# Forgetting attention of a hybrid decoder step: prompt scores made in two layouts, with a pair's row maxima fetched one pair ahead

## What is computed

```python
s = jnp.einsum('bqhd,bkhd->bhqk', qb, k, preferred_element_type=F32) * scale
s = s + jnp.swapaxes(cqb, 1, 2)[..., :, None] - ckT[:, :, None, :]
s = jnp.where((kpos[None, :] <= qpb[:, None])[None, None], s, -jnp.inf)
p = jax.nn.softmax(s, axis=-1)
return jnp.einsum('bhqk,bkhd->bqhd', p.astype(v.dtype), v)
...
y = (o * jax.nn.silu(z)).astype(h.dtype) @ w_out
```

## Time and profile before

| | us |
|---|---|
| median of three runs (lowest, highest) | 2239.72 (2234.27, 2247.66) |
| profiled execution | 2248.77 |
| its span, first to last instruction | 2247.0 |
| TensorE busy in the span | 1930.5 (86%) |
| VectorE, ScalarE, POOL busy | 1129.9, 563.5, 349.8 |
| mean granted clock of TensorE | 0.907 |

### The profile page before, as it was taken

How to read it: one execution, slowest core, us unless ns; L and a number is a source line. 1 busy time by engine, 2 the same in 40 slices (tenths; PEclk the granted TensorE clock), 3 DMA queues, 4 the chain that set the end, 5 groups by cost and what they waited for, 6 DMA issues and landing times. The chain is left out here.

```text
span 2247.0 us, 39897 instructions
## 1 busy us (share of the span) xinstructions
PE 1930.5 (86%) x15120; PEld 1416.0 (63%) x15120; DVE 1129.9 (50%) x1810; ACT 563.5 (25%) x1253; POOL 349.8 (16%) x401
## 2 busy tenths in 40 slices
PE   4999999999999788999999996877877768768798
PEld 3876877777787566877877774544444434344475
DVE  4444534544563687677677763333334333333423
ACT  4211121121121421111111111333433334233431
POOL 0000000000000034544445442011011010110010
PEclk9999999999999898999999997568889788687899
DMA  4111111111111479999999997247678676685761
GB/s 136 38 44 48 43 40 56 35 49 47 39 49 38 161 232 308 343 312 341 348 325 330 317 323 253 105 154 248 218 212 258 224 233 225 203 257 181 276 243 71
DMA packets 218393, 413.65 MB, mean 184 GB/s; under 512 B 18593, under 2 KB 129858, under 8 KB 218014
## 3 DMA queue, kind: packets, MB, share of 16 engines
q1 hardware_dynamic: 148764, 222.15, 30.6%
q0 software_dynamic: 51648, 180.71, 23.5%
q10 hardware_dynamic: 17874, 9.27, 1.4%
HBM read 370.85 MB, written 41.94 MB: 184 GB/s over the span
## 5 line engine op out<-in xcount | busy, mean ns | idle before, releaser
L1180 DVE STREAM_TRANSPOSE kt<-k_raw 128x1024 f32<-128x1024 f32 x256 | 310.8, 1234 | 145.7 <-DMA k_raw<-in_cache_k_dram,k_idx 120.0
L347 POOL DMA_INDIRECT k_raw<-in_cache_k_dram,k_idx x256 | 259.4, 1013 | 444.4 <-DVE kt L1180 284.6
L765 PE MATMUL ps_a<-h_hi,w_hi 128*128 128x512 f32 x656 | 265.7, 405 | 1.7 <-DVE w_lo L1017 1.7
L766 PE MATMUL ps_a<-h_lo,w_hi 128*128 128x512 f32 x656 | 258.7, 394 | 0.0
L767 PE MATMUL ps_a<-h_hi,w_lo 128*128 128x512 f32 x656 | 258.6, 394 | 0.0
L1693 DVE TENSOR_REDUCE pp_nm<-ps_a 128x1 f32<-128x128 f32 (+3 forms) x64 | 48.5, 758 | 306.4 <-PE ps_a L1421 306.4
L1017 DVE TENSOR_TENSOR w_lo<-w_raw,w_hi 128x1024 fp32r<-128x1024 f32 x97 | 109.1, 1124 | 171.3 <-ACT w_hi L594 169.0
L1443 PE MATMUL b<-con,p_p 128*128 128x128 f32 x432 | 98.4, 347 | 102.7 <-DVE p_p L1701 48.4
L765 PE MATMUL ps_b<-h_hi,w_hi 128*128 128x512 f32 x384 | 157.2, 409 | 0.0
L766 PE MATMUL ps_b<-h_lo,w_hi 128*128 128x512 f32 x384 | 152.1, 396 | 0.0
L767 PE MATMUL ps_b<-h_hi,w_lo 128*128 128x512 f32 x384 | 152.0, 396 | 0.0
(11 more groups left out here) (291 smaller groups left out, 3131.8 us busy)
## 6 DMA issues: line engine op xcount, KB each, us to landing
v_pg<-in_cache_v_dram SPq DMA_DIRECT2D x256, 512.0 KB, 5.1
w_raw<-in_w_in_pool_dram SPq DMA_DIRECT2D x32, 512.0 KB
w_raw<-in_w_in_attn_dram SPq DMA_DIRECT2D x32, 512.0 KB
w_raw<-in_w_out_pool_dram SPq DMA_DIRECT2D x16, 512.0 KB
s_scr<-ss_st ACTq DMA_DIRECT2D x64, 128.0 KB
s_in<-s_scr POOLq DMA_DIRECT2D x16, 512.0 KB, 5.0
d_sb<-decay POOLq DMA_DIRECT2D x32, 256.0 KB, 6.9
z_scr<-x_st SPq DMA_DIRECT2D x8, 528.0 KB, 4.6
```

Of the source, the lines that this page charges most:

```text
L347: pool.indirect_dma_start(k_raw[:, k, :], None, cache_rows, bass.IndirectOffsetOnAxis(ap=k_idx[:, u, k:k + 1], axis=0)).then_inc(k_full[k] ...
L765: nc.tensor.matmul(ps, ah, bh, start=j == 0, stop=False)
L766: nc.tensor.matmul(ps, ah, bl, start=False, stop=False)
L1180: V.transpose(kt[u % 2][:, :, 32 * k:32 * k + 32], k_raw[:, k, :].rearrange("p (i c) -> p i c", c=32)).then_inc(dve_kt, 1)
```

## The change

- The scores of a pair are made twice. `query_rows` makes them as before, queries on partitions, only for the row maxima, and one pair ahead: while pair `b` is worked, the rows of pair `b + 1` are made and reduced (`row_max`, `max_columns`). `keys_turned` makes them with keys on partitions, with a 67th row that adds the negated maximum of each query; ScalarE's `prompt_exp` is then an exponential without bias or sum, and its result `pt_x` is at once the moving operand of `prompt_values`. `QBLOCKS`, `prompt_turn`, `prompt_evac` and `prompt_norm` are gone.
- The steps go over key blocks 0 to 7; step `s` has the queries from 128 s on, in parts of up to 512 columns. Both kinds of scores pass through a ring of four banks. The values' sums stand in `o_ps` (two banks) for the whole pair.
- The maxima get into the query tile by `max_row`: TensorE turns 16 columns of maxima (`max_turn`), ScalarE copies them, stores them to DRAM and loads them as row 66 of the query tile of the next pair. Both DMAs are on ScalarE's queue.
- The row sums: VectorE adds the key blocks' weights (`part_sums`), a product with ones sums over partitions (`row_sums`, twice a pair), and `gate` takes a reciprocal of 512 columns and multiplies twice.
- Sample `b` is worked in pair `b`, so all eight pairs have one, and the output projection has none. Before pair 0 stand its maxima and the scores of its sample. The last pair makes no rows.
- Queries, keys and values of a pair have two buffers; POOL loads those of pair `b + 1` as pair `b` begins. SP loads `w_o` after page 3 of the last pair. At the end ScalarE splits all of `w_o` before the first of `z_t`. In the first block the last stores of SP stand ahead of the first eight value pages.

```diff
-QBLOCKS = (0, 7, 1, 6, 2, 5, 3, 4)
...
+    nm_d = internal("nm_d", (16, P))
...
+        pt_x = [[place(f"pt_x{h}{i}", [P, SEQ], F32, big_at(2048 * h + 1024 * i)) for i in range(2)] for h in range(2)]
+        acc = [place(f"acc{h}", [P, SEQ], F32, big_at(4096 + 1024 * h)) for h in range(2)]
...
+        o_ps = ps_a
+        ring = (ps_b[:, 0:512], ps_b[:, 512:1024], ps_c[:, 0:512], ps_c[:, 512:1024])
+        M_SLOTS = ((), (0, 1), (2,), (3, 4), (5,), (6,), (7,), ())
+
+
+        def turned(s):
+
+            return [(h, a, e) for h in range(2) for a, e in ((P * s, 512), (max(512, P * s), SEQ)) if a < e]
+
+        def row_parts(m):
+
+            return [(h, a, e) for h in range(2) for a, e in ((0, min(512, P * m + P)), (512, P * m + P)) if a < e]
+
+        T_AT = [sum(len(turned(i)) for i in range(s)) for s in range(SLOTS + 1)]
+        M_AT = [sum(len(row_parts(i)) for i in range(m)) for m in range(SLOTS + 1)]
+        N_T, N_M = T_AT[SLOTS], M_AT[SLOTS]
...
+                for p in range(PAGES):
+                    v_page(NB - 1, p)
+                    if p == 3:
+                        sp.wait_ge(pe_t, N_T * (NB - 1))
+                        sp.wait_ge(dve_s, N_S * NB)
+                        for k in range(KT8):
+                            sp.dma_start(w_o[k][:, :], w_out_attn[0, P * k:P * k + P, :]).then_inc(w_full[k], 16)
...
                 for b in range(NB):
-                    for s in range(SLOTS):
-                        if s == 0 and b > 0:
-                            pool.wait_ge(dve_s, b * N_S)
+                    if 0 < b < NB - 1:
+                        pool.wait_ge(pe_t, N_T * b)
+                        hold(pool)
+                        qk_pair(pool, b + 1)
+                        pool.wait_ge(pe_pvp, SLOTS * b)
+                        hold(pool)
+                        v_pair(pool, b + 1)
+                    if b:
+                        sample_out(b - 1)
+                    if b < NB - 2:
+                        for half in range(2):
+                            pool.wait_ge(dve_s, N_S * (b + 1) + 2 * half + 2)
                             hold(pool)
-                            score_half(b, 1)
-                        if s == 1 and b > 1:
-                            sample_out(b - 1)
-                        if s == 4 and b < NB - 1:
-                            pool.wait_ge(dve_s, b * N_S + 2)
-                            hold(pool)
-                            score_half(b + 1, 0)
-                        if s == 6 and b < NB - 1:
-                            pool.wait_ge(pe_s, b * 16 + 16)
-                            hold(pool)
-                            qk_pair(pool, b + 1)
-                        if s == 7 and b < NB - 1:
-                            pool.wait_ge(pe_pvp, b * SLOTS + SLOTS)
-                            hold(pool)
-                            v_pair(pool, b + 1)
-
-                pool.wait_ge(pe_new, NB)
-                for i in range(3):
+                            score_half(b + 2, half)
...
+                def keys_turned(b, par, s, uses):
+
                     if s == 0:
-                        pe.wait_ge(ld_qk, b * 32 + 32)
-                    first, last = score_columns(s)
+                        pe.wait_ge(ld_nm, b * 16 + 16)
+                    for i, (h, a, e) in enumerate(turned(s)):
+                        j = uses.index(("t", T_AT[s] + i))
+                        ring_wait(b, uses, j)
+                        diag = a == P * s
+                        out = ring[j % 4]
+                        mm = nc.tensor.matmul(out[:, 0:e - a], ka[par][:, h, P * s:P * s + P], qa[par][:, h, a:e],
+                                              start=True, stop=not diag)
+                        if diag:
+                            mm = nc.tensor.matmul(out[:, 0:P], caus_b[:, :], ident_b[:, :], start=False, stop=True)
+                        mm.then_inc(pe_t, 1)
+
+                def query_rows(b, par, m, uses):
+
+                    for i, (h, a, e) in enumerate(row_parts(m)):
+                        j = uses.index(("m", M_AT[m] + i))
+                        if uses is ROWS_FIRST:
+                            if j >= 4:
+                                pe.wait_ge(dve_mx, j - 3)
+                        else:
+                            ring_wait(b - 1, uses, j)
+                        diag = e == P * m + P
+                        out = ring[j % 4]
+                        mm = nc.tensor.matmul(out[:, 0:e - a], qa[par][0:AUG, h, P * m:P * m + P], ka[par][0:AUG, h, a:e],
+                                              start=True, stop=not diag)
+                        if diag:
+                            mm = nc.tensor.matmul(out[:, e - a - P:e - a], ident_b[:, :], caus_b[:, :], start=False, stop=True)
+                        mm.then_inc(pe_m, 1)
...
+                def prompt_values(b, par, s):
+
+                    pe.wait_ge(act_p, b * N_T + T_AT[s + 1])
+                    if s == 0:
+                        pe.wait_ge(ld_v, b * 16 + 16)
+                        past(pe, dve_g, b * 2)
+                    for a, e in ((P * s, 512), (max(512, P * s), SEQ)):
+                        if a < e:
+                            for h in range(2):
+                                r = HD * h
+                                mm = nc.tensor.matmul(o_ps[r:r + HD, a:e], v_pr[par][:, s, r:r + HD], pt_x[h][s % 2][:, a:e],
+                                                      start=s == 0, stop=s == (3 if e == 512 else 7), tile_position=(0, r))
+                    mm.then_inc(pe_pvp, 1)
...
+                def pair(b, par, first, last):
+                    uses = USES_LAST if last else USES_ALL
                     for s in range(SLOTS):
                         if s == 0:
-                            scores(b, 0)
+                            if not first:
+                                prompt_values(b - 1, 1 - par, SLOTS - 1)
+                            keys_turned(b, par, 0, uses)
                         else:
-                            prompt_values(b, s - 1)
-                        if sample and s % 2 == 0:
-                            sample_turn(b, s // 2)
-                        if sample and s == SLOTS - 1:
+                            keys_turned(b, par, s, uses)
+                            prompt_values(b, par, s - 1)
+                        if not last:
+                            if s == 1:
+                                pe.wait_ge(ld_qk, b * 32 + 64)
+                            for m in M_SLOTS[s]:
+                                query_rows(b + 1, 1 - par, m, uses)
+                        if s % 2 and s < SLOTS - 1:
+                            sample_turn(b, (s + 1) // 2)
+                        if s == 4:
+                            row_sums(b, 0)
+                        if s == 5:
                             new_turn(b)
-                        prompt_turn(b, s, 0)
-                        prompt_turn(b, s, 1)
-                        if sample:
-                            sample_values(b, s)
-                        if s < SLOTS - 1:
-                            scores(b, s + 1)
-                    new_scores(b)
-                    prompt_values(b, SLOTS - 1)
+                        if s == 6 and not last:
+                            new_scores(b + 1, False)
+                        if s == SLOTS - 1 and not last:
+                            max_turn(b + 1)
+                        sample_values(b, s)
+                        if s == SLOTS - 1 and not last:
+                            sample_turn(b + 1, 0)
+                        if s == 0 and not first:
+                            row_sums(b - 1, 1)
...
+                pe.wait_ge(ld_qk, 32)
+                for m in range(SLOTS):
+                    query_rows(0, 0, m, ROWS_FIRST)
+                new_scores(0, True)
+                max_turn(0)
                 pe.wait_ge(ld_ls, 16)
-                batch(0, False)
-                with pe.Fori(1, NB) as b:
-                    batch(b, True)
+                sample_turn(0, 0)
+                pair(0, 0, True, False)
+                with pe.Fori(0, NB // 2 - 1) as i:
+                    pair(i * 2 + 1, 1, False, False)
+                    pair(i * 2 + 2, 0, False, False)
+                pair(NB - 1, 1, False, True)
...
+                def prompt_exp(b, s, uses):
+                    past(act, pe_pvp, b * SLOTS + (s - 1))
+                    past(act, dve_ps, b * SLOTS + (s - 1))
+                    for i, (h, a, e) in enumerate(turned(s)):
+                        j = uses.index(("t", T_AT[s] + i))
+                        act.wait_ge(pe_t, b * N_T + (T_AT[s] + i + 1))
+                        nc.scalar.activation(pt_x[h][s % 2][:, a:e], ring[j % 4][:, 0:e - a], ACT.Exp).then_inc(act_p, 1)
+
+                def max_row(b, par):
+                    act.wait_ge(pe_nm, b + 1)
+                    past(act, ld_nm, b * 16)
```

(45 more changed lines are left out.)

545 lines of the change are left out of this document (259 added, 286 removed).

## The result

The change makes the kernel slower. After: 2315.03 us median of 4 runs (2312.40 to 2316.79); before, on the same chip: 2236.99 us (2230.98 to 2247.66). The ratio is 1.034, with a 95% interval of 1.030 to 1.0385. The forecast was 2159 us, with a range of 2095 to 2232; the result lies above the range.

What follows compares the result with a forecast made beforehand. No engine was full; waits in one chain and halved clock took 35 of 89.0 us a pair. Start 1391.8, first maxima 51.6, pair 0 84, six pairs 462, pair 7 57.4, last stretch 118.5: 2165.3, scaled to 2159; range 2095 to 2232.

Steps and rivals of the forecast that it cites:

- the one on DMA: Loads per pair: same traffic plus a row of keys, needed 15 to 20 us after issue, landing in 15.2; charged nothing.
- Slower by the landings: Rival, maxima's DMAs: landings like the sample's output rows' 10.4 us add 12.8 in seven pairs and the start, 2261; chance 0.03.
- Value products: TensorE, per pair: products in instructions of 512 columns take 10.5 us, between 8.6 side by side and 17.9 one after the other.
- Heads do not overlap: Rival, wide products: no overlap (+7.4 and +1.5), or landings of 5.3 us; a pair of 85, 2215 us; chance 0.18.
- The round trip: Maxima over DRAM between pairs: two landings of 4 us, copy and issues, 8.6 us (3.9 to 11.2); TensorE idles 4.5.
- Clock after it: Pair's first scores after the maxima's wait: half clock until pages and row sums have run, 5 us charged (0 to 10).
- I charge nothing: VectorE, per pair: reductions, sums and two reciprocals (1.4 to 11 us) keep it at 40 to 50 of 77 us, covered.
- An inner pair: Each of six middle pairs: 67.5 us of work, 4.5 of idle and 5 of slow clock, 77 us.
- better: Rival, each pair: landings about 2 us and the clock holds or returns on scores; 70 us a pair, 2110; chance 0.17.
- nothing gained: Rival, score banks: TensorE waits for VectorE or ScalarE to empty them; 88 to 89 us a pair, about 2240; chance 0.05.
- slower by the clock: Rival, inside each pair: clock drops and scores never raise it; half clock for half a pair, about 2370; chance 0.10.
- No wait for keys or pages: Sign of being right, within pairs: TensorE waits for neither key loads nor cache pages.

Runs made afterwards that it cites:

- e1: The changed kernel with a pair's keys loaded by two transfers, 66 rows and then the row of ones, instead of one of 67; 2202.1 us, 0.983 of before.
- e3: The changed kernel with 68 rows in the keys' load, still one transfer; 2237.8 us, 0.999 of before.
- e12: e9 with the row of ones loaded only for pairs 0 and 1; 2161.3 us, 0.965 of before.
- e6: e1 with the last maxima made a step earlier and the sample's exponentials made before the wait for the landing; 2217.0 us, 0.989 of before.
- e5: e1 with the row sums of the second half of the queries taken before the pair's first scores; 2176.9 us, 0.9695 of before.
- e9: e5 with maxima turned right behind step 6's pages, sent earlier, and the sample's exponentials before the wait for the landing; 2166.5 us, 0.967 of before.
- e10: e9 with the three attention loops over pairs written out; 2160.7 us, 0.966 of before.
- e7: e1 with the edits of both e5 and e6; 2205.1 us, 0.985 of before.
- e4: The changed kernel with 80 rows in the keys' load, still one transfer; 2232.8 us, 0.9975 of before.
- e8: e7 with the three attention loops over pairs written out; 2195.8 us, 0.981 of before.

## Why the prediction was wrong

**The step that failed** is the one on DMA: "It is the same traffic, plus a row of keys. Keys come one pair ahead, issued at the end of a pair and needed some 15 to 20 us later, against 15.2 to landing. Charged nothing". I priced the row by its bytes, 1.5% more, and took the old landing time for the new load. The row changed how the load is spread: one engine in place of eleven, 42.5 us in place of 15.2. The time from issue to need was also wrong, on the safe side: in the trace of after it is some 33 us (1626.3 to 1659.2, where TensorE begins to wait), and the load outlasts even that by 12. It had no rival either. "Slower by the landings" was about the maxima's small transfers, and none of the rivals had a wait for keys, though I had named that wait as the largest DMA wait of before.

What it cost can be read between after and e1, which differ in that load alone. By the profiled spans, 2315.1 and 2198.4: 116.7 us. The start takes 21.4 of them (1409.9 against 1388.5): pair 0's keys go out ahead of the last cache keys of the stage before, and VectorE's longest wait for these is 25.5 us in after and 9.2 in e1. The start also varies without such a load, from 1387.9 to 1397.6 us in the traces of e1 and e3 to e12, so the keys' part in it may be 12 to 22 us. The six inner pairs take 591.5 - 494.9 = 96.6, of which 77.7 are idle time of TensorE (124.4 against 46.7) and 18.9 are slower work, at a clock of 0.81 against 0.88. The rest is within 2 us.

**The other steps**, on e1, where the keys are out of the way. Its span is 33.1 us above the 2165.3 of my sum:

```profile
1388.50:1438.90 50.40, 36.00 (x86) 17.38 (x87) 21.17 (x47) 2.63 (x6) 11.09 (x17) 0.50 0.68 241
1438.90:1520.45 81.55, 71.45 (x485) 31.84 (x484) 38.85 (x76) 19.56 (x51) 8.86 (x14) 0.88 0.70 222
1520.45:2015.35 494.90, 448.15 (x2922) 195.94 (x2923) 248.23 (x439) 113.98 (x300) 47.03 (x74) 0.88 0.73 247
2015.35:2073.00 57.65, 53.58 (x394) 21.25 (x394) 19.24 (x21) 17.05 (x44) 1.13 (x2) 0.88 0.87 319
2073.00:2198.40 125.40, 105.51 (x476) 78.65 (x472) 53.97 (x73) 28.66 (x44) 11.45 (x21) 0.89 0.18 66
```

- Start 1388.5 for 1391.8; maxima of pair 0 50.4 for 51.6; pair 0 81.6 for 84; pair 7 57.7 for 57.4. Right, 7 us better in all.
- Value products: right that heads overlap. The first four products of a pair, 512 columns each and so sixteen blocks, take 1540.79 - 1538.92 = 1.87 us in e6's order of time, so 72 blocks 8.4 us a pair for the 10.5 charged. "Heads do not overlap" is out. Row sums: 1.0 us each, 2.0 a pair for 2.5.
- The round trip: 8.6 us forecast; the first landing takes 3.7 (median of e1) for 4. Idle 4.5 forecast; 5.7 in e1, of which 2.1 are the loop's jumps. Right.
- Clock after it: the first scores of a pair do run at half clock in e1, about 0.5 us a block in the order of time above, and the clock is back at the first pages' end, at 1610 us. Right, as far as that wait goes.
- VectorE "I charge nothing": wrong. The cover named, four score banks, was the right one for the maxima, but the reciprocal sits in another chain, between row sums and the value products of the next step. It costs 1.7 us idle in each pair and slow work behind it: 2.9 us a pair between e1 and e5. It is in the last stretch too, where TensorE waits 8.1 us for a chain of the row sums' reciprocal, two products and the casts of `z_t`; how much of the stretch's error that makes was not tried. The last stretch took 125.4 for 118.5.
- An inner pair of e1 is 82.5 us for 77: 74.7 of work for 72.5, and 7.8 of idle for 4.5. With e5's and e9's edits it is 77.0: 72.6 of work (435.39 / 6) and 4.4 of idle. The sum of the parts was right, but for an order of work that keeps the reciprocal off the path.
- The forecast of 2159 us is what e12 and e10 reach. That is luck and no merit of it: they have edits that the forecast did not know, and the changed kernel as given is 156 us slower.
- Rivals: "better" and "nothing gained" did not happen, and "slower by the clock" neither, as a cause of its own: with half of a pair's 67.5 us of work at half clock the pair's mean clock would be 0.67, and it is 0.81 in after and 0.88 in e1. But its sign, half clock inside a pair, did show, in e1 once in each pair behind the wait for the reciprocal: the clock falls there after a wait, and 18.9 us of the 116.7 are such slow work behind the keys' wait. "No wait for keys or pages" was named as a sign of being right; after has both waits, and they led to the cause.

## What to carry to other kernels

Before a transfer's shape is changed, even by one row, ask how many DMA engines its outer dimension can be spread over: here the prime number 67 put all of it on one, and the cache pages, which have a part on every engine, were late with it. A constant row goes into a transfer of its own, or is loaded once. And when a wait is taken away or work is moved between steps, ask which loads it was covering: in e6 the wait at the pairs' ends fell by 30 us and that for pages grew by 38.

## What was not expected of the hardware

- POOL's issue of the load takes 2.17 us with 67 rows, 1.01 with 68, 0.63 with 80.
- The reciprocal on VectorE: 3358 ns for 128x512.
- After, e1, e5 and e9 have idle times of 4 to 7 us at the two jumps of TensorE's loop of two pairs, which wait for nothing that the profile shows and go when the loop is written out (`PE ps_a L1455 <- issue: 12.7, 2, 7.2` in e1). The kernel before, with a loop of one pair, has none. e6 and e7 have the same loop of two pairs and only 2.2 and 1.7 us of it. That instructions are brought in there again fits, but was not shown, nor why it costs so little in those two.

Two things stay open. Why the DMA engines are fuller at the moment of the maxima's store in e3 and e4 than in e1 was not tried. And whether the late pages of e6 to e8 come from the bus or from their ring of eight tiles, no run tells apart: the stretch 1585 to 1605 us of e6 has a DMA share of 0.76, so the bus had room on average.
